# Memory keys and values computed ahead of the first feed-forward, with eleven rooms for the first adaptation pieces and a reordered spatial gate

## The chip, the cores and the metric

The kernel runs on one NeuronCore of a Trainium2 chip. The metric is the device time of one execution in microseconds, and lower is better. Five engines work beside each other, each in the order of its own program, and wait for one another on semaphores: TensorE (PE) multiplies matrices, VectorE (DVE) and ScalarE (ACT) do elementwise work, GpSimd (POOL) prepares and issues the loads of the weights, SyncE (SP) issues the other transfers.

## The reference

The input is x of 512 tokens with 1024 features. Everything is float32.

```
mod = silu(c) @ ada_w + ada_b                    # 1024 -> 6 * 1024: shift, scale and gate, twice
h = rms_norm(x, g) * (1 + sc1) + sh1
p = h @ w_in                                     # inputs and gates of four mixers
merged = sum(gate_i * mixer_i)                   # rwkv7, spatial gating, short convolution, s5
x = x + gt1 * (merged @ w_o)
h = rms_norm(x, g) * (1 + sc2) + sh2
x = x + gt2 * (square(relu(h @ ffn_w1)) @ ffn_w2)     # 1024 -> 4096 -> 1024
x = rms_norm(x, final_g)
for layer in 0, 1:                               # forget attention, then dilated attention with rope
    mn = rmsnorm(mem, norm_mem[layer])           # mem: 256 tokens x 1024, an input
    km, vm = split(mn @ w_mem_kv[layer])         # 4 memory heads of 64, keys and values
    heads = concat(attention of 12 heads over x, attention of 4 heads over km, vm)
    x = x + heads @ w_out[layer]
    x = x + conv_ffn(rmsnorm(x, norm_ffn[layer]))     # 1024 -> 2 * 2816, convolution, 2816 -> 1024
y = rmsnorm(x, norm_final)
```

`mn` depends on the input `mem` and on no `x`.

## The kernel before

Activations lie transposed: features on the 128 partitions, the 512 tokens along the row. A product is made from three matmuls, high half times high half, high times low, and low times high. The weights come as pieces of 128 x 1024 in one stream of 334. A tile is the product of one piece with eight blocks of 128 features: 24 matmuls of 512 columns into one PSUM bank, of which four are in turn. `project(tiles, owner, ...)` issues tiles, and waits for the low half of each piece and for the bank to be read.

The weight stream has four slots. For each piece q, GpSimd waits for the high half, writes its negative to the low slot (L448), issues a load that adds the full weights to it (L451), and then issues the high half of piece q + 2 (L442). That one waits until TensorE has begun piece q - 1. GpSimd does all this in order, so the low half of the next piece is issued behind that wait.

The adaptation weights are 48 pieces of 512 KB, in six groups of eight (`modulate(group, a, b)`, L576 and L578, multiplies and adds pieces on VectorE; `modulation(group)`, L1682, sums over the partitions on TensorE with 8 matmuls of one column). Pieces 0 to 3 are taken by TensorE itself (L1690). Groups 0 and 1 are needed before the first norm, group 2 before the x update, 3 and 4 around it, 5 in the first feed-forward. SyncE loads them in order into rings of rooms: eight rooms for pieces 0 to 15, four later.

In the run-up, VectorE computes the tables of the s5 mixer: `f` as six products of 128 x 1024 (L1009 to L1014), then group 0, the reciprocal, group 1, and the norm (`norm`, L538 and L534). TensorE transposes `f` (L1850) and multiplies it with `c_in` (L1855) before the first `project`. After the first ten tiles (convolution and spatial gate inputs) the spatial gate has a layer norm: sums on TensorE (L1873), a root on ScalarE (L1356), reciprocal and scaling on VectorE (L1103 to L1106), transposes on TensorE (L1879). The short convolution and group 2 stand on VectorE ahead of it, and small s5 tables of up to 512 columns (L1076 to L1092). The s5 scan is fed at L1899 and read at L1912.

Around the first feed-forward: `last_terms(mixer_update)` updates x as the eight w_o tiles end (L1188) with two adaptation multiplies beside each; ScalarE squares (L1266), TensorE sums (L1698), ScalarE takes the root (L1268), VectorE norms.

The memory in each layer: the memory input is loaded, squared and summed beside the last group of the feed-forward before it. Behind the tiles `memq0 memq1 q0 k0 v0` of the attention stand `memk0 memk1 memv0 memv1`, each with 256 columns. VectorE makes their operand in 24 instructions (L836, L483, L484). Values come out transposed, are copied by ScalarE (L1310), turned by TensorE (`turn`, L1711, bank 7) and taken by VectorE (L822). Then `attention(layer)` starts with unit 0, whose scores are the first memory pair (L1782), reduced on VectorE (L890). The attention's 32 units share TensorE with the remaining q, k, v tiles.

## Time and profile before

| | |
|---|---|
| median of 3 runs | 2261.84 us (2259.82 to 2265.03) |
| profiled execution | 2262.56 us, span 2260.7 us |
| mean granted TensorE clock | 0.968 |
| TensorE busy | 2124.0 us (94%) |
| VectorE busy | 1296.8 us (57%) |
| ScalarE busy | 455.7 us (20%) |
| GpSimd busy | 841.6 us (37%) |
| moved by DMA | 389.34 MB, 172 GB/s in the mean |

Busy time says what an engine was occupied with, not that the end depended on it. The chain that ended last, followed back from the end, is 77% TensorE, 14% VectorE and 6% DMA. Durations of matmuls are modelled and overlap: the distance between starts is what one costs. A granted clock of 1.00 is 2.4 GHz, 0.50 is 1.2 GHz.

### The profile page before, as it was taken

Reading aid. Unit: us, or ns where it says so; the run is one execution under the profiler, and the core shown is the slowest. Engines: PE = TensorE matmul, PEld = TensorE weight load, DVE = VectorE, ACT = ScalarE, POOL = GpSimd, SP = SyncE. Lnnn points to the kernel's source line nnn. Section 1 sums busy time; section 2 is a strip of 40 time slices with the busy share of each in tenths; the row PEclk is TensorE's granted clock in tenths of the full one; section 3 lists DMA queues with packets and bytes.
Section 4 is the critical chain, followed back from the end, with each engine's and each line's share of the span. In section 5 each row is a group of like instructions: output and inputs, shape, how many; then the busy total and the mean of one; then the engine's idle time right before and its main releaser. Section 6 shows DMA issues by size and latency. Waiting matters only on the chain.

```text
span 2260.7 us, 27381 instructions
## 1 busy us (share of the span) xinstructions
PE 2124.0 (94%) x10790; PEld 1684.3 (75%) x10790; DVE 1296.8 (57%) x1827; ACT 455.7 (20%) x839; POOL 841.6 (37%) x1009
## 2 busy tenths in 40 slices
PE   6989799998799999998999999999989989999996
PEld 5768587776588888876777888888766768888885
DVE  6775646437653243684444754727746657727374
ACT  2112301220100000313333211202224342202021
POOL 1323233233244444442223444444432224444442
PEclk7999899999799999999999999999999999999998
DMA  8867567579799888875556888988964549889885
GB/s 289 229 139 170 112 142 165 114 168 234 210 241 198 190 193 195 190 170 119 110 103 162 186 192 198 186 197 171 200 135 99 112 90 195 189 196 197 190 187 127
DMA packets 121783, 389.34 MB, mean 172 GB/s; under 512 B 25220, under 2 KB 27396, under 8 KB 121272
## 3 DMA queue, kind: packets, MB, share of 16 engines
q0 software_dynamic: 96624, 346.27, 70.6%
q1 hardware_dynamic: 25032, 41.32, 5.5%
q8 instruction: 86, 1.41, 0.3%
q14 instruction: 41, 0.34, 0.0%
HBM read 383.67 MB, written 3.92 MB: 171 GB/s over the span
## 4 chain that ended last, share of the span: by engine, by line
PE 77%; DVE 14%; DMA 6%; issue 1%; ACT 1%; POOL 0%; SPq 0%; DVEq 0%; ACTq 0%
PE ps L1617 64%; DMA w_lo<-in_w 2%; DMA arena<-in_ada 2%; PE ps L1646 2%; PE ps L1782 2%; PE ps L1811 2%; PE ps L1797 1%; DVE work L690 1%; PE ps L1969 1%; DVE g_lo L484 1%; PE ps L1733 1%; DVE arena L691 1%; DVE arena L578 1%; DMA w_hi<-in_w 1%; DVE small L890 0%
## 5 line engine op out<-in xcount | busy, mean ns | idle before, releaser
L1617 PE MATMUL ps<-h_hi,w_hi 128*128 128x512 f32 x1760 | 711.8, 404 | 27.3 <-DVE h_lo L534 13.1
L1617 PE MATMUL ps<-h_hi,w_lo 128*128 128x512 f32 x1760 | 690.3, 392 | 0.0
L1617 PE MATMUL ps<-h_lo,w_hi 128*128 128x512 f32 x1760 | 690.2, 392 | 0.0
L442 POOL DMA_DIRECT2D w_hi<-in_w x334 | 186.3, 558 | 1218.1 <-PE ps L1617 1082.9
L1617 PEld LDWEIGHTS ps<-h_hi,w_hi 128*128 128x128 f32 x1760 | 333.0, 189 | 125.5 <-issue 29.9
L1617 PEld LDWEIGHTS ps<-h_hi,w_lo 128*128 128x128 f32 x1760 | 332.8, 189 | 71.5
L1617 PEld LDWEIGHTS ps<-h_lo,w_hi 128*128 128x128 f32 x1760 | 333.8, 190 | 65.0 <-issue 2.2
L448 POOL TENSOR_SCALAR w_lo<-w_hi 128x1024 fp32r<-128x1024 f32 (+1 forms) x334 | 355.6, 1065 | 67.1 <-DMA w_hi<-in_w 61.8
L451 POOL DMA_DIRECT2D w_lo<-in_w x334 | 300.9, 901 | 106.0 <-POOL w_lo L448 106.0
L1617 PE MATMUL ps<-g_hi,w_hi 128*128 128x512 f32 (+1 forms) x760 | 297.1, 391 | 10.3 <-DMA w_lo<-in_w 6.3
L1617 PE MATMUL ps<-g_lo,w_hi 128*128 128x512 f32 (+1 forms) x760 | 291.1, 383 | 0.0
L1617 PE MATMUL ps<-g_hi,w_lo 128*128 128x512 f32 (+1 forms) x760 | 291.0, 383 | 0.0
L1617 PEld LDWEIGHTS ps<-g_hi,w_hi 128*128 128x128 f32 x760 | 144.8, 191 | 43.9 <-DMA w_lo<-in_w 9.2
L1617 PEld LDWEIGHTS ps<-g_hi,w_lo 128*128 128x128 f32 x760 | 144.7, 190 | 27.8
L1617 PEld LDWEIGHTS ps<-g_lo,w_hi 128*128 128x128 f32 x760 | 144.9, 191 | 26.6 <-issue 0.5
L1575 ACT ACTIVATE arena<-arena,vec 128x512 f32<-128x512 f32 x88 | 71.8, 816 | 392.1 <-DVE arena L936 388.8
L950 DVE TENSOR_TENSOR x<-ps,x 128x512 f32<-128x512 f32 x48 | 33.2, 692 | 146.0 <-PE ps L1617 135.8
L941 DVE SCALAR_TENSOR_TENSOR arena<-arena,vec 128x511 f32<-128x511 f32 x88 | 114.9, 1305 | 3.3 <-ACT arena L1575 0.3
L936 DVE TENSOR_TENSOR arena<-ps,work 128x512 f32<-128x512 f32 x88 | 60.8, 691 | 90.3 <-PE ps L1617 88.9
L1205 DVE TENSOR_TENSOR arena<-arena 128x512 f32<-128x512 f32 x32 | 54.3, 1696 | 70.6 <-ACT arena L1496 70.6
L1213 DVE SCALAR_TENSOR_TENSOR x<-ps,mod,x 128x512 f32<-128x512 f32 x32 | 24.0, 751 | 101.9 <-PE ps L1617 101.7
L483 DVE CAST g_hi<-arena 128x512 fp32r<-128x512 f32 (+1 forms) x100 | 75.5, 755 | 3.4
(376 smaller groups left out, 2109.3 us busy)
## 6 DMA issues: line engine op xcount, KB each, us to landing
w_hi<-in_w POOLq DMA_DIRECT2D x318, 512.0 KB, 3.9
w_lo<-in_w POOLq DMA_DIRECT2D x318, 512.0 KB, 5.6
arena<-in_ada SPq DMA_DIRECT2D x40, 512.0 KB, 9.4
w_hi<-in_w POOLq DMA_DIRECT2D x16, 384.0 KB, 3.4
w_lo<-in_w POOLq DMA_DIRECT2D x16, 384.0 KB, 5.1
x<-in_ada SPq DMA_DIRECT2D x8, 512.0 KB, 7.9
x<-in_xT SPq DMA_DIRECT2D x1, 2048.0 KB, 9.5
x<-in_xT SPq DMA_DIRECT2D x4, 512.0 KB, 5.3
```

Source lines behind the costliest of these rows:

```text
L442: pool.dma_start(w_hi[:, q % SLOTS, 0:n], A["w"][q][:, 0:n]).then_inc(S(f"high_in{q % SLOTS}"), 16)
L448: pool.tensor_scalar(w_lo[:, q % SLOTS, 0:n], w_hi[:, q % SLOTS, 0:n].bitcast(F32), -1.0, 0.0, ALU.mult, ALU.add).then_inc(S("negated"), 1)
L451: pool.dma_start(w_lo[:, q % SLOTS, 0:n], A["w"][q][:, 0:n], accum_op=ALU.add).then_inc(S(f"low_in{q % SLOTS}"), 16)
L483: do(dve.tensor_copy(hi, src))
L936: do(dve.tensor_tensor(cv_m["z"][:, side, :], tile()[:], rstd, ALU.mult), "conv_scaled")
L941: do(dve.scalar_tensor_tensor(dst[:, 1:], z[:, :T - 1], w(1), dst[:, 1:], ALU.mult, ALU.add))
L1205: do(dve.tensor_tensor(s, r, r, ALU.mult), "relu_used")
L1575: do(act.activation(c[:, j % 2, :], cv_m["z"][:, side, :], ACT.Identity, scale=V("cw2", at), bias=V("cb2", 44 * layer + 22 * side + j0 + j ...
L1617: mm = pe.matmul(bank, w[:, slot, cols], a(k), start=(k == 0 and i == 0), stop=(k == blocks - 1 and i == 2))
L1646: mm = pe.matmul(banks[i], w[:, slots[i], cols], a(k), start=(k == 0 and j == 0), stop=(k == blocks - 1 and j == 2))
L1782: mm = pe.matmul(ps[2 + g][:, 0:width], at_m["q"][half(g), pair, P * qb:P * qb + P], keys, start=True, stop=not fox)
L1811: mm = pe.matmul(ps[6][64 * g:64 * g + 64, P * qb:P * qb + P], values, at_m["pt"][:, u % 2, g, P * b:P * b + P], start=(b == 0), stop=(b = ...
```

## The change

Three things change.

The memory's norm, keys and values of both layers are computed between the x update and the first feed-forward. Eight pieces of `w_mem_kv` move there in the weight stream, and the pieces per layer fall by four. The norm is factored: only the gain is applied to the operand (ScalarE makes the high half, `mem_high`, VectorE the low half, `memory_low`, in `mixer_update`), the root's reciprocal multiplies the keys afterwards (`mem_scaled`, in the first feed-forward group) and the values as they are copied (`mem_row`, its transposed form). Values are computed with the memory as the stationary operand (`memory_values`), so that they come out with tokens on the partitions and are not turned. The memory input is loaded once, behind adaptation pieces 24 to 27.

The first adaptation pieces get eleven rooms; pieces 11 to 15 wait for VectorE to have used the room. The products `f` and the s5 transposes and products move behind the first norm.

The convolution, group 2 of the adaptation and its sum move behind the spatial gate's sums. Group 2's last four pieces are loaded behind the s5 input's transfers.

VectorE, from the s5 tables to the second adaptation group (L10xx are products of 1024 columns, L576 and L578 multiply adaptation pieces, L527 is the norm's reciprocal). Before:

```order
L1012 TENSOR_TENSOR arena<-arena 128x1024
L1013 TENSOR_TENSOR arena<-arena 128x1024
L1014 TENSOR_TENSOR arena<-arena 128x1024
L1033 TENSOR_SCALAR arena<-arena 128x128
L576 TENSOR_SCALAR arena<-arena,small 128x1024
L578 SCALAR_TENSOR_TENSOR arena<-arena,small 128x1024 x3
L580 MEMSET small 128x8
L527 RECIPROCAL work<-work 128x512
L576 TENSOR_SCALAR arena<-arena,small 128x1024
L578 SCALAR_TENSOR_TENSOR arena<-arena,small 128x1024 x7
L580 MEMSET small 128x8
L587 TENSOR_TENSOR mod<-ps,vec 128x16
```

Of the change (L595 and L597 multiply adaptation pieces, L546 is the reciprocal, L557 the norm):

```order
L1007 TENSOR_TENSOR arena<-arena 128x8x4
L595 TENSOR_SCALAR arena<-arena,small 128x1024
L597 SCALAR_TENSOR_TENSOR arena<-arena,small 128x1024 x3
L599 MEMSET small 128x8
L595 TENSOR_SCALAR arena<-arena,small 128x1024
L597 SCALAR_TENSOR_TENSOR arena<-arena,small 128x1024 x7
L599 MEMSET small 128x8
L546 RECIPROCAL work<-work 128x512
L606 TENSOR_TENSOR mod<-ps,vec 128x16
L1032 SCALAR_TENSOR_TENSOR small<-mod,vec 128x8
```

The six products and `c_in`'s sign are gone from this place, and the reciprocal follows the second group.

ScalarE, from the root of the rwkv norm to the first feed-forward tile (L1382 gates, L1266 squares of x, L1268 root, L1274 the norm's high half, L1496 relu). Before:

```order
L1483 ACTIVATE small<-small 128x16
L1382 ACT_TABLE_LOAD
L1382 ACTIVATE arena<-ps 128x512 x4
L1259 ACT_TABLE_LOAD
L1259 ACTIVATE small<-small 128x1
L1266 ACTIVATE work<-x 128x512 x8
L1268 ACTIVATE work<-ps,small 128x512
L1274 ACTIVATE h_hi<-work,mod 128x512 x8
L1496 ACTIVATE arena<-ps 128x512 x25
```

Of the change (L1269 squares of x, L1271 root, L1309 copies keys, L1315 copies values, L1512 the norm's high half, L1524 relu; the 24 activations of the memory norm stand ahead of these rows):

```order
L1262 ACTIVATE small<-small 128x1
L1269 ACTIVATE work<-x 128x512 x8
L1271 ACTIVATE work<-ps,small 128x512
L1309 ACTIVATE arena<-ps 128x256 x2
L1315 ACTIVATE arena<-ps,small 128x256 x2
L1512 ACTIVATE h_hi<-work,mod 128x512 x2
L1309 ACTIVATE arena<-ps 128x256
L1512 ACTIVATE h_hi<-work,mod 128x512 x2
L1309 ACTIVATE arena<-ps 128x256
L1512 ACTIVATE h_hi<-work,mod 128x512 x4
L1315 ACTIVATE arena<-ps,small 128x256 x2
L1524 ACTIVATE arena<-ps 128x512 x32
```

Copies of keys and values now stand between the high halves of the norm.

VectorE, from the memory's last eviction to the first unit of layer 0 (L820 and L822 take turned values, L853 copies keys, L858 to L867 the forget sums, L890 the first score reduction). Before, with the 24 rows of the memory norm ahead of these:

```order
L820 COPY arena<-ps 128x4x128
L853 COPY arena<-ps 128x256
L858 TENSOR_SCALAR work<-work 12x512
L859 TENSOR_TENSOR work<-work 12x512
L860 MEMSET work 12x512
L861 SCALAR_TENSOR_TENSOR work<-work 12x512
L864 CAST work<-work 12x512
L865 TENSOR_TENSOR work<-work 12x512
L866 CAST work<-work 12x512
L867 TENSOR_TENSOR work<-work 12x512
L822 COPY arena<-ps 128x2x128 x2
L890 TENSOR_REDUCE small<-ps 128x2
```

Of the change (L815 the scaled memq0, memq1, q0 and k0, L857 to L866 the forget sums, L832 the scaled v0, L887 the reduction):

```order
L815 SCALAR_TENSOR_TENSOR arena<-ps,work 128x512 x4
L857 TENSOR_SCALAR work<-work 12x512
L858 TENSOR_TENSOR work<-work 12x512
L859 MEMSET work 12x512
L860 SCALAR_TENSOR_TENSOR work<-work 12x512
L863 CAST work<-work 12x512
L864 TENSOR_TENSOR work<-work 12x512
L865 CAST work<-work 12x512
L866 TENSOR_TENSOR work<-work 12x512
L832 TENSOR_TENSOR arena<-ps,work 128x512
L887 TENSOR_REDUCE small<-ps 128x2
L893 RECIPROCAL small<-small 128x2
```

Nothing of the memory is left between the scaled tiles and the first reduction.

```diff
-ADA_PE, ADA_FIRST = 4, 8
+ADA_PE, ADA_FIRST = 4, 11
...
             for q in range(16):
-                if ADA_FIRST <= q < ADA_FIRST + ADA_PE:
-                    sp.wait_ge(S("ada_taken"), q - ADA_FIRST + 1)
-                elif q >= ADA_FIRST + ADA_PE:
-                    sp.wait_ge(S("ada_used"), q - ADA_FIRST - ADA_PE + 1)
-                sp.dma_start(first_slots[q % ADA_FIRST], A["ada"][q]).then_inc(S(ada_landed(q)[0]), 16)
+                if q >= ADA_FIRST:
+                    sp.wait_ge(S("ada_used"), q - ADA_FIRST + (3 if q == 15 else 1))
+                sp.dma_start(first_slots[first_room(q)], A["ada"][q]).then_inc(S(ada_landed(q)[0]), 16)
...
+            for q in range(16 + ADA, 24):
+                ada_piece(q, ada_second["ada"])
...
             def memory_root():
+
                 need("rms_ready")
                 do(dve.reciprocal(mem_rstd, mem_rstd))
+                for i in range(2):
+                    do(dve.tensor_tensor(mem_m["diag"], mem_rstd[:, P * i:P * i + P], K("ident"), ALU.mult))
+                    do(dve.tensor_reduce(mem_row[:, i:i + 1], mem_m["diag"], AX.X, ALU.add), "mem_row")
+
+            def memory_low(i):
+
+                layer, k = i // KT, i % KT
+                need("mem_high")
+                do(dve.scalar_tensor_tensor(mn(g_lo, layer, k), mem_in[:, k, :], V("g_mem2", 8 * layer + k), mn(g_hi, layer, k).bitcast(F32),
+                                            ALU.mult, ALU.subtract), "mem_ready")
...
-                value_scaled("v0")
-                for i in range(NMP):
-                    do(dve.tensor_copy(km[:, i, :], tile()[:, 0:MT]), "dve_freed")
-                    if i == 0:
-                        value_taken("v0")
                 if layer == 0:
                     need("forget_log")
                     do(dve.tensor_scalar(f(0), f(0), 0.0, None, ALU.min))
@@ -865,9 +864,7 @@
                     do(dve.tensor_tensor(f(3), f(4), f(0), ALU.subtract))
                     do(dve.tensor_copy(part(1), f(3)))
                     do(dve.tensor_tensor(part(2), f(3), f(1), ALU.subtract), "forget_parts")
-                skip(2)
-                for i in range(NMP):
-                    value_taken(f"memv{i}")
+                value_scaled("v0")
 
...
-            do(dve.tensor_scalar(c_in[:, 1], c_in[:, 1], -1.0, None, ALU.mult), "s5_f")
             n.next("square", KT)
             n.next("square_used", KT)
             modulate(0, ADA_PE, 8)
+            modulate(1, 0, 8)
             norm_start()
-            modulate(1, 0, 8)
             modulation(0, 2)
             gain1 = small[:, 2, :]
             do(dve.scalar_tensor_tensor(gain1, mod[:, 8:16], 1.0, V("g_mix", 0, 8), ALU.add, ALU.mult))
             norm(lambda k: gain1[:, k:k + 1], lambda k: mod[:, k:k + 1])
...
 
             skip(4)
-            modulation(2)
             need("sg_sums")
             d = m["z"][:, 2:4, :]
             do(dve.tensor_scalar(m["mu"], PA[:], 1.0 / DM, None, ALU.mult))
             for k in range(2):
                 do(dve.tensor_tensor(d[:, k, :], d[:, k, :], m["mu"], ALU.subtract))
                 do(dve.tensor_tensor(m["sq"][:, k, :], d[:, k, :], d[:, k, :], ALU.mult), "sg_square")
...
+            convolved(1)
             shifted(1)
             for k in range(2):
                 need("sg_mixed")
...
 
             count = [0]
 
@@ -1161,6 +1155,9 @@
             do(dve.tensor_tensor(w[:, 1, :], w[:, 1, :], w[:, 3, :], ALU.add), "s5_states")
             for i in range(3, 7):
                 shifted(i)
+                if i < 6:
+                    modulate(2, 2 * (i - 2), 2 * (i - 2) + 2)
+            do(dve.tensor_tensor(mod[:, 16:24], tile()[:, 0:8], V("ada_b", 16, 8), ALU.add), "dve_freed")
...
             def mixer_update(k):
                 do(dve.scalar_tensor_tensor(x[:, k, :], tile()[:], mod[:, 16 + k:17 + k], x[:, k, :], ALU.mult, ALU.add), "x_done")
+                for i in range(3 * k, min(3 * k + 3, 2 * KT)):
+                    memory_low(i)
+                if k == 2:
+                    memory_root()
...
-                    if last:
-                        add_square(j, mem_sq, mem_total)
+                    if first and j < 2 * NMP:
+                        keys = mem_keys[j // NMP][:, j % NMP, :]
+                        dve.wait_ge(S("mem_copied"), 2 * N_KV)
+                        do(dve.tensor_tensor(keys, keys, mem_rstd, ALU.mult), "mem_scaled")
                 if first:
                     modulation(5)
                 update = lambda k: do(dve.scalar_tensor_tensor(x[:, k, :], tile()[:], mod[:, 40 + k:41 + k], x[:, k, :],
...
+            for k in range(KT):
+                if k >= MEM_SQ:
+                    act.wait_ge(S("mem_square_used"), k - MEM_SQ + 1)
+                do(act.activation(mem_sq(k), mem_in[:, k, :], ACT.Square), "mem_square")
+            act.wait_ge(S("tile"), n.value["tile"])
+            for layer in range(2):
+                for k in range(KT):
+                    do(act.activation(mn(g_hi, layer, k), mem_in[:, k, :], ACT.Identity, scale=V("g_mem2", 8 * layer + k)), "mem_high")
+            act.wait_ge(S("mem_square_used"), KT)
+            do(act.activation(mem_rstd, PB[:, 0:MT], ACT.Sqrt, bias=small[:, 38, 0:1], scale=1.0 / D), "rms_ready")
             skip(8)
             rms_x(0)
-            high_shifted(lambda k: mod[:, 24 + k:25 + k])
+            for i in range(NMP):
+                keys_copy(0, i)
+            values_copy(0)
+
+            def high2(k):
+                need("norm_scaled")
+                do(act.activation(h_hi[:, k, :], work[:, 4 + k % 2, :], ACT.Identity, bias=mod[:, 24 + k:25 + k]), "h_high")
+
+            for k in range(KT):
+                high2(k)
+                if k in (1, 3):
+                    keys_copy(1, k // 2)
+            values_copy(1)
             for g in range(FF_GROUPS):
...
+            def memory_values(layer):
+
+                at = [bank_of(t[0] + i) for i in range(2)]
+                for b in at:
+                    pe.wait_ge(S(freed[b][0]), freed[b][1])
+                for k in range(KT):
+                    if k % 4 == 0:
+                        slot = open_piece()
+                    hi, lo = mn(g_hi, layer, k), mn(g_lo, layer, k)
+                    cols = slice(MT * (k % 4), MT * (k % 4) + MT)
+                    for i in range(2):
+                        tokens = slice(P * i, P * i + P)
+                        for j, (a, w) in enumerate(((hi, w_hi), (hi, w_lo), (lo, w_hi))):
+                            mm = pe.matmul(ps[at[i]][:, 0:NMP * P], a[:, tokens], w[:, slot, cols], start=(k == 0 and j == 0),
+                                           stop=(k == KT - 1 and j == 2))
+                            if k % 4 == 0 and i == 0 and j == 0:
+                                mm.then_inc(S("w_used"), 1)
+                        if k == KT - 1:
...
-                    mm = pe.transpose(ps[i][:, P * s:P * s + P], m["f"][:, i // 2, 4 * (i % 2) + s, :], K("ident"))
+                    mm = pe.transpose(ps[4 + i][:, P * s:P * s + P], m["f"][:, i // 2, 4 * (i % 2) + s, :], K("ident"))
                 mm.then_inc(S("s5_turned"), 1)
+            project(1, "dve_freed")
+            pe.wait_ge(S("s5_e"), 4)
             for s in range(S5T):
                 for part in range(2):
                     for g in range(2):
                         mm = pe.matmul(ps[6 + g][:, 16 * s:16 * s + 16], m["f"][halves[g], part, s, :], m["c_in"][halves[g], part, s, :],
                                        start=(part == 0), stop=(part == 1))
             mm.then_inc(S("s5_products"), 2)
-            modulation(0)
-            modulation(1)
-            pe.wait_ge(S("s5_e"), 4)
-            project(10, ["dve_freed"] * 6 + ["act_freed"] * 4, ready=h_tile)
-            modulation(2)
+            project(6, ["dve_freed"] * 2 + ["act_freed"] * 4)
 
...
             branch_out(3, 8)
+            for k in range(KT):
+                pe.wait_ge(S("mem_square"), k + 1)
+                pe.matmul(PB[:, 0:MT], K("ones"), mem_sq(k), start=(k == 0), stop=(k == KT - 1)).then_inc(S("mem_square_used"), 1)
             project(7, "x_done", ready=lambda k: need("merged"))
             modulation(3)
             project(1, "x_done")
+            memory = [(lambda k: mn(g_hi, 0, k), lambda k: mn(g_lo, 0, k)), (lambda k: mn(g_hi, 1, k), lambda k: mn(g_lo, 1, k))]
+            pe.wait_ge(S("mem_ready"), 2 * KT)
+            project(1, "mem_copied", operand=memory[0], width=MT)
             modulation(4)
+            total_squares(work[:, 2, :])
+            project(NMP - 1, "mem_copied", operand=memory[0], width=MT)
+            memory_values(0)
+            project(NMP, "mem_copied", operand=memory[1], width=MT)
+            memory_values(1)
             g = (of(g_hi), of(g_lo))
             hidden = lambda k: need("hidden")
-            total_squares(work[:, 2, :])
             for group in range(FF_GROUPS):
                 project(8, "hidden_relu", ready=h_tile if group == 0 else None)
                 project(2, "x_done", operand=g, ready=hidden)
                 if group == 0:
...
                 project(1, "v_scaled")
                 if layer:
                     turn("k0", layer)
-                project(1, "dve_freed", operand=mem, width=MT, ready=lambda k: need("mem_ready"))
-                turn("v0", layer)
-                project(NMP - 1, "dve_freed", operand=mem, width=MT)
-                for i in range(NMP):
-                    project(1, "v_copied", operand=mem, width=MT)
-                    if i:
-                        turn(f"memv{i - 1}", layer)
-                turn(f"memv{NMP - 1}", layer)
-                attention(layer)
+                attention(layer, ready)
...
```

## Rows read from the trace of the kernel before

**Rows 1.** The chain that ended last, in order of time (start us, us, what)

```profile
168.35 2.08 PE ps L1899 x64
...
185.05 3.72 PE ps L1912 x64
...
490.72 8.18 DMA w_lo<-in_w
...
666.11 261.30 PE ps L1617 x1152
...
1005.84 4.67 PE ps L1617 x24
```

**Rows 2.** Timeline of DVE, 20 to 50 us (start, us, instruction, idle before)

```profile
20.30 1.23 DVE L1009 TENSOR_TENSOR arena<-arena 128x1024 f32<-128x1024 f32 x1
...
48.80 1.63 DVE L578 SCALAR_TENSOR_TENSOR arena<-arena,small 128x1024 f32<-128x1024 f32 x1 [1.42 <-DMA arena<-in_ada]
```

**Rows 3.** DMA rate, 0 to 60 us in 40 slices

```profile
GB/s 0 204 377 327 328 360 385 396 415 415 418 426 404 366 76 14 22 284 169 224 235 249 336 265 317 371 394 360 276 259 391 356 237 266 374 258 206 186 182 193
```

**Rows 4.** PE: its waits in total (us, times, longest), and timeline, 30 to 146 us

```profile
PE ps L1617 <- DMA w_lo<-in_w: 12.0, 10, 2.0
...
32.27 3.66 PE L1850 MATMUL ps<-con,arena 128*128 128x128 f32 x16
35.85 7.01 PE L1855 MATMUL ps<-arena 64*128 64x16 f32 x64
...
119.89 1.84 PE L1682 MATMUL ps<-con,work 128*128 128x1 f32 x16
...
141.82 3.78 PE L1873 MATMUL ps<-arena,con 128*128 128x512 f32 x4 [7.28 <-DVE arena L1101]
```

**Rows 5.** Timeline of DVE, 103 to 184 us

```profile
103.02 0.49 DVE L1062 TENSOR_SCALAR arena<-arena,vec 128x512 f32<-128x512 f32 x1
...
112.71 0.69 DVE L484 TENSOR_TENSOR g_lo<-arena,g_hi 128x512 fp32r<-128x512 f32 x1
...
139.33 0.07 DVE L1092 MEMSET arena<- 128x8 f32 x1
...
183.01 0.69 DVE L1161 TENSOR_TENSOR arena<-arena 128x512 f32<-128x512 f32 x1
```

**Rows 6.** Busy time by stretch (us; PE, PEld, DVE, ACT, POOL; PEclk, DMA, GB/s)

```profile
587.00:615.30 28.30, 16.60 (x42) 10.15 (x43) 21.65 (x26) 7.09 (x10) 2.50 (x3) 0.58 0.48 136
545.00:587.00 42.00, 40.03 (x181) 32.29 (x179) 28.68 (x29) 4.44 (x7) 16.93 (x20) 0.99 1.02 309
```

**Rows 7.** Timeline of ACT, 596 to 616 us

```profile
596.49 0.69 ACT L1268 ACTIVATE work<-ps,small 128x512 f32<-128x512 f32 x1 [8.06 <-PE ps L1698]
...
615.56 0.60 ACT L1496 ACTIVATE arena<-ps 128x512 f32<-128x512 f32 x1 [1.97 <-PE ps L1617]
```

**Rows 8.** Timelines of POOL and PE, 1643 to 1654 us

```profile
1643.39 0.56 POOL L442 DMA_DIRECT2D w_hi<-in_w  x1 [4.97 <-PE ps L1617]
...
1651.09 0.39 PE L1617 MATMUL ps<-g_hi,w_hi 128*128 128x256 f32 x1 [1.64 <-DMA w_lo<-in_w]
...
1653.94 0.28 PE L1617 MATMUL ps<-g_hi,w_lo 128*128 128x256 f32 x1
```

**Rows 9.** Timelines of PE and DVE, 997 to 1022 us

```profile
997.78 0.28 PE L1617 MATMUL ps<-g_hi,w_hi 128*128 128x256 f32 x1
...
1011.06 1.77 DVE L858 TENSOR_SCALAR work<-work 12x512 f32<-12x512 f32 x1
...
1018.02 0.68 DVE L867 TENSOR_TENSOR work<-work 12x512 fp32r<-12x512 f32 x1
...
1021.73 0.69 DVE L890 TENSOR_REDUCE small<-ps 128x2 f32<-128x512 f32 x1 [1.48 <-PE ps L1782]
```

**Rows 10.** Timelines of PE and DVE, 1634 to 1658 us

```profile
1634.13 1.02 PE L1708 MATMUL ps<-arena,con 128*128 128x512 f32 x2
...
1657.16 0.69 DVE L890 TENSOR_REDUCE small<-ps 128x2 f32<-128x512 f32 x1 [1.09 <-PE ps L1782]
```

199 lines of the change are left out of this document (97 added, 102 removed).

## The prediction

> **What bounds the kernel now.** I read the chain of waits in order of time first. Long stretches of it are nothing but TensorE: 1152 matmuls of 512 columns in 261.3 us, so 0.227 us each and 5.44 us for a tile of 24 [rows 1]. There the time is fixed, and only pieces taken out of the program could shorten it. The change takes none out of these stretches; it moves work between the places where TensorE waits. So the sum is made from the waits, place by place, with the timelines of the engines beside each other. Four places matter: the run-up to the first norm, the gap before the first feed-forward, and the starts of the two attentions.
>
> **A. First norm.** VectorE computes six products of 1024 columns from 20.30 to 27.9 us before it touches the first adaptation piece; the last multiply starts at 48.80 and waited for its DMA [rows 2]. In the data rates of the first 60 us the DMA falls idle once (76, 14, 22 GB/s at slices 15 to 17 of 1.5 us), and runs at 240 to 430 else [rows 3]: with eight rooms pieces 8 to 11 wait for TensorE to have taken pieces 0 to 3. With eleven rooms nothing waits there, and since the products move behind the norm, rooms 4 to 7 come free from about 22 us. Bytes that must have moved by the last piece: 8.4 MB of pieces, 2.1 of x, 1.4 of constants, and 1.6 of weights that come between; 13.5 MB at some 390 GB/s from 3 us on end near 38 us, and with the multiply the sum stands at 39.5 instead of 50.4: 11 us earlier. Bounds: VectorE alone (12 multiplies of 1.3 from 20.3) would give 36, so 14 us; the old ring's pace gives 45, so 5.
>
> What TensorE did while it waited now stands between tiles: 16 transposes (3.66) and 64 small products (7.01) [rows 4], both at the half clock level in that row's stretch; warm I take half, 5.4 us. TensorE's waits for low halves are ten in the whole program, 12.0 us, the longest 2.0 [rows 4]; two of them lay here, 1.9 us, and can go, since only four of the eight next adaptation pieces still compete. The tenth tile ended at 119.9, where the adaptation sum starts [rows 4]: 119.9 - 11 + 5.4 - 1.9 = 112.4.
>
> **Spatial gate.** TensorE waited 7.28 us at 141.82 for VectorE, and ran the sums in 3.78, the half level [rows 4]. VectorE was late because two convolutions (103.0 to 113.4, 5.2 each) and eight adaptation multiplies stood ahead of its 26 us of small tables, which ended at 139.3 [rows 5]. Without them it ends near 117. So TensorE goes 112.4, tile, 1.9 us of sums, tile, 1.9 us of sums: 127.1 where it was 145.6, 18.5 ahead. The root, reciprocal and transposes follow as before; the second convolution (5.2) now stands ahead of the mixing, and I find VectorE done with it at 150.0 where TensorE's scan inputs started at 168.35 [rows 1], 18.2 ahead. Given back: two multiplies (2.4) go ahead of the scan, of which 1.3 is covered (VectorE's last step ended at 183.7, TensorE used it at 185.05 [rows 1, 5]), and the adaptation sum, 1.84 [rows 4], moves behind. **A = -15.3 us**, between -9 and -19.
>
> **B. Memory input.** 1 MB more is queued near 487 us, where the load of a low half takes 8.18 us on the chain [rows 1]: +1. Eight squares are summed on TensorE. Two sums of 512 columns took 3.78 at the half level [rows 4], so eight of 256 warm take 3.8 us. They run while the first w_o tile waits for its merged parts, and cost nothing; without that cover, +3.8. ScalarE and VectorE work of this norm (24 activations, 16 subtractions) lies beside the update of x, where VectorE is busy 28.7 of 42 us and the DMA share is 1.02 [rows 6]; 10 us more just fits. If it doesn't, up to 3 us, kept in the range.
>
> **C. The memory pieces before the feed-forward.** TensorE is busy 16.6 of the 28.3 us from 587.0 to 615.3, at a granted clock of 0.58 [rows 6]. The adaptation sums and the squares are done when ScalarE takes the root at 596.49, and the first feed-forward tile is read at 615.56 [rows 7]. Eight short pieces now go in. One takes 2.9 us warm (1651.09 to 1653.94 and its own 0.28) [rows 8]. TensorE's need is thus 23 us, and would nearly fit. But the weights do not come so fast: GpSimd asks for a high half at 1643.39 when a piece begins, only then issues the next low half, and TensorE waits until 1651.09 for it [rows 8]. With 0.5 us from the piece's start to the issue, a piece starts no sooner than 8.2 us after the piece two before it. Piece 0 starts at 587.0, piece 1 behind the adaptation sum and the squares at 596.4, then 599.3, 604.6, 607.5, 612.8, 615.7, 621.0, and the first feed-forward tile at 623.9. ScalarE copies the results out in between and its last normed part is ready near 623, so that tile runs at full pace and ends at 629.3. **C = +14 us.** Bounds: 0, if the feed keeps up and fully hides; +22, if cold (below).
>
> **D. Attention, layer 0.** TensorE had the last value tile at 997.78; the first score reduction on VectorE was at 1021.73 [rows 9]. In between lay four memory pieces, 24 norm steps and two transposed copies. What is late next: VectorE's forget sums, 1011.06 to 1018.70, 7.6 us [rows 9], now directly behind the fourth scaled tile. That tile ends near 992.4, so 993.3 + 7.6 + 0.7 for the value tile = 1001.8: 19.9 earlier. The value's four transposes (0.9, a quarter of the 16 in 3.66 [rows 4]) move into the attention, where TensorE is the bound. **D = -19.0.** If the value tile's eviction made the attention's tiles wait, -16.
>
> **E. Attention, layer 1.** The second rotation ran on TensorE at 1634.13; the first reduction was at 1657.16 [rows 10]. Now rotation (2.2) and value scaling (0.7) follow it, and the reduction comes at 1637.6: 19.5 earlier, less 0.9. **E = -18.6**, at least -15.
>
> **F.** Two sums of squares of 256 columns go, 0.5 us each by the same row: **-1**. Masks and rope tables keep their places in the DMA queue.
>
> **Sum.** -15.3 + 1 + 14 - 19.0 - 18.6 - 1 = -38.9. The profiled execution took 2262.56, 1.9 more than its span; 2262.56 - 38.9 = **2224**. The median of the three runs is 2261.84, 0.7 less; I leave it at that.
>
> **Rivals.** *Cold feed.* The short pieces run at the half level: 24 of them took 4.67 us with part at half level [rows 1], 5.1 if all. Then seven pieces from 596.4 end at 632.1, and the next tile at 638: C = 22.5, time 2232. For it: a granted clock of 0.58 in that stretch. Against: after a wait of 1.64 us the piece at 1651.09 ran at full level [rows 8]. The Trainium skill, "TensorE: Matmul & The Clock Gate", section "HAM oscillation — how this bites in real kernels", says that bursts shorter than the weight waits between them start cold every time. By that rule C is this rival's; by the row it is mine. The row at 1651.09 speaks against the rule so far, and its stretch had fewer waits than this one will.
>
> *The front gives little.* The last adaptation piece lands at 45 and VectorE remains last at the scan: A = -5, time 2234. For it: the weights' first loads compete at 40 us. Against: the idle slices.
>
> *Memory fully hidden.* The feed keeps TensorE's pace, C = 0: 2210. Against: the 1.64 us that a short piece waited for its low half [rows 8].
>
> *Slower.* In C nothing overlaps: each of six pieces from 599.3 on pays the 8.2 of the feed, its own 2.9, and 0.5 more, since with adaptation pieces on the DMA a low half alone can take 8.18 us [rows 1]. At 11.6 a piece the first feed-forward tile starts at 668.9 and ends at 674.3: C = +59, time 2269. It decides from 10.6 us a piece, where C eats the other 52.9. For it: the last adaptation pieces load just then, 4 MB. Against: the low half asked for after 1643.39 was there at 1651.09 though the one before it had been on its way [rows 8], so two overlap.
>
> **Chances.** Forecast 0.55 (alone 2216 to 2231), cold feed 0.15, weak front 0.12, hidden 0.12, slower 0.04; 0.02 that it all comes to nothing. The range takes the hidden case's edge and both middle rivals: 2208 to 2242. Less than 0.2% (4.5 us) cannot be told from no change. Faster 0.94, same 0.02, slower 0.04.
>
> **What would show it.** The last adaptation multiply ends near 39.5; the wait of 7.28 for VectorE is gone; the scan inputs start near 150. Between the last update of x and the first feed-forward tile TensorE runs eight short pieces with waits for low halves of 2 to 3 us before every second one, and the second feed-forward tile starts 14 us later in relation to the x updates. The first score reduction follows the last value tile's end by some 4 us in both layers. It is wrong if the stretches between (feed-forward, down products, recurrence) change their lengths, or if the attentions take longer than 1.1 us more each.

## The result and the profile after

| | before | after |
|---|---|---|
| first comparison, medians | 2260.83 us (4 runs) | 2243.31 us (2242.19 to 2249.14, 4 runs) |
| ratio | | 0.9928, interval 0.9902 to 0.9953 |
| second comparison | 2265.17 us (9 runs) | 2241.46 us (2240.33 to 2244.40, 4 runs) |
| ratio | | 0.9896, interval 0.9882 to 0.9910 |
| profiled executions | 2262.56 us | 2249.14 and 2240.72 us |

The change is faster by 17 to 24 us. The forecast was 38 us, and its range ended at 2242, below the first median and above the second. The sign was right; the size forecast was 1.6 to 2.2 times the measured one.

The page of the changed kernel, its first profiled execution:

```profile
span 2247.3 us, 27332 instructions
PE 2122.3 (94%) x10794; PEld 1686.9 (75%) x10794; DVE 1273.4 (57%) x1778; ACT 462.0 (21%) x850; POOL 844.9 (38%) x1009
DMA packets 121639, 388.29 MB, mean 173 GB/s; under 512 B 25204, under 2 KB 27380, under 8 KB 121256
```

Bytes and shares are nearly those of before (1.05 MB less, since the memory input is loaded once), so they do not tell where the time went; the chain of waits does. The chain of after, in order of time (start us, us, what), to be read against [rows 1]:

```profile
155.44 2.08 PE ps L1949 x64
172.17 3.72 PE ps L1962 x64
482.59 11.10 DMA w_lo<-in_w
493.73 7.32 PE ps L1633 x24
604.14 8.22 DMA w_lo<-in_w
615.03 7.65 DMA w_lo<-in_w
625.72 7.22 DMA w_lo<-in_w
691.00 293.94 PE ps L1633 x1296
```

The reader is to see two things. The scan inputs (168.35 before) start 12.9 us earlier, and the long run of the feed-forward (666.11 before) starts 24.9 us later. Between them stand four loads of low halves. The 1296 matmuls of that long run take 293.94 us, 0.227 each as before.

By stretches, each measured between the same two events of TensorE in both traces (us; the last column is the change once more):

| stretch | before | after | difference | forecast | again |
|---|---|---|---|---|---|
| start to the solve's first product behind its DMA (A) | 377.56 | 368.16 | -9.4 | -15.3 | -14.1 |
| to the recurrence's last product | 108.80 | 110.07 | +1.3 | 0 | +0.2 |
| to the output's transposes, past the low half near 490 (B) | 18.25 | 22.76 | +4.5 | +1 | +5.7 |
| to the adaptation's last sum (C) | 86.29 | 91.41 | +5.1 | 0 | +4.9 |
| to the adaptation sum in the feed-forward (C) | 73.37 | 96.76 | +23.4 | +14 | +21.5 |
| to the sum of squares ahead of layer 0's feed-forward (D) | 581.44 | 557.39 | -24.1 | -19.5 | -24.2 |
| to that of layer 1 (E) | 640.43 | 624.39 | -16.0 | -19.1 | -16.5 |
| to the end | 374.56 | 376.36 | +1.8 | 0 | +0.6 |

The forecast's F is split over D and E. The stretches of the two layers gave together what was forecast: -40.1 against -38.6. The start gave 3.5 us less in the mean of its two executions (the thirteen profiled kernels with this start stand between -7.1 and -14.1 at this event, -10.3 in the mean). The stretch around the memory pieces cost 28.5 and 26.4 us where 14 stood, and B 3.5 and 4.7 more than forecast. That is nearly all of the miss.

The memory pieces on TensorE, their first matmuls, and the first feed-forward tile (start us, us, instruction, idle before):

```profile
592.40 3.58 PE L1701 MATMUL ps<-con,arena 128*128 128x1 f32 x16 [7.68 <-DVE small L599]
596.90 1.20 PE L1633 MATMUL ps<-g_hi,w_hi 128*128 128x256 f32 x1
601.54 0.28 PE L1737 MATMUL ps<-w_hi,g_hi 128*128 128x256 f32 x1
612.40 0.39 PE L1633 MATMUL ps<-g_hi,w_hi 128*128 128x256 f32 x1 [3.32 <-DMA w_lo<-in_w]
622.82 0.36 PE L1737 MATMUL ps<-w_hi,g_hi 128*128 128x256 f32 x1 [2.65 <-DMA w_lo<-in_w]
632.99 0.50 PE L1633 MATMUL ps<-h_hi,w_hi 128*128 128x512 f32 x1 [2.70 <-DMA w_lo<-in_w]
```

The second piece starts at 596.90, the first feed-forward tile at 632.99: 36.1 us for seven pieces (35.8 in the other execution), 10.2 to 10.9 for two. Before, that tile began at 603 and its result was read at 615.56 [rows 7]; now ScalarE reads it 24.9 us later:

```profile
640.46 0.60 ACT L1524 ACTIVATE arena<-ps 128x512 f32<-128x512 f32 x1 [9.43 <-PE ps L1633]
```

GpSimd in that stretch: the high half that waits for the piece at 601.54, the negation of the next piece, and the issue of its low half, which lands at 612.36. Below it is the busy time from 612 to 623 and in the whole row of pieces (us; PE, PEld, DVE, ACT, POOL; PEclk, DMA share, GB/s):

```profile
602.13 0.55 POOL L450 DMA_DIRECT2D w_hi<-in_w  x1 [0.88 <-PE ps L1737]
602.70 1.14 POOL L456 TENSOR_SCALAR w_lo<-w_hi 128x1024 fp32r<-128x1024 f32 x1
604.14 0.89 POOL L459 DMA_DIRECT2D w_lo<-in_w  x1 [0.30 <-POOL w_lo L456]
...
612.00:623.00 11.00, 7.88 (x49) 7.41 (x50) 6.28 (x8) 3.37 (x6) 5.02 (x6) 0.84 1.00 206
601.50:633.00 31.50, 21.40 (x147) 20.32 (x145) 15.38 (x18) 8.82 (x15) 15.11 (x18) 0.89 0.95 204
```

The order of the steps is the forecast's. The landing is not: 8.22, 7.65 and 7.22 us where [rows 8] showed 5.7. The DMA engines are busy nearly all the time (share 0.95, and 1.00 from 612 to 623) at only 204 to 206 GB/s.

VectorE in the attentions' heads, the first score reduction in layer 0 and in layer 1, answering [rows 9] and [rows 10]:

```profile
1025.28 0.69 DVE L887 TENSOR_REDUCE small<-ps 128x2 f32<-128x512 f32 x1
...
1639.32 0.69 DVE L887 TENSOR_REDUCE small<-ps 128x2 f32<-128x512 f32 x1
```

### The profile page after: what moved, and what is told of

Same layout as the page of the kernel before. It is cut to its first block, busy times and chain, and to the rows that moved or that the text cites. A ratio compares the mean times of both kernels' runs of the same rounds, so it can differ in the third digit from the quotient of the medians.

```text
span 2247.3 us, 27332 instructions
## 1 busy us (share of the span) xinstructions
PE 2122.3 (94%) x10794; PEld 1686.9 (75%) x10794; DVE 1273.4 (57%) x1778; ACT 462.0 (21%) x850; POOL 844.9 (38%) x1009
## 3 DMA queue, kind: packets, MB, share of 16 engines
q0 software_dynamic: 96624, 346.27, 72.4%
## 4 chain that ended last, share of the span: by engine, by line
PE 79%; DVE 10%; DMA 7%; issue 1%; ACT 1%; POOL 1%; SPq 0%; DVEq 0%; ACTq 0%
PE ps L1633 65%; DMA w_lo<-in_w 4%; PE ps L1662 2%; PE ps L1830 2%; PE ps L1859 2%; PE ps L1845 1%; DMA w_hi<-in_w 1%; DMA arena<-in_ada 1%; PE ps L2020 1%; DVE work L709 1%; PE ps L1778 1%; POOL w_lo L456 1%; DVE arena L710 1%; DMA x<-in_xT 1%; PE ps L1701 1%
## 5 line engine op out<-in xcount | busy, mean ns | idle before, releaser
L1633 PE MATMUL ps<-g_hi,w_hi 128*128 128x512 f32 (+1 forms) x728 | 287.2, 395 | 8.7 <-DMA w_lo<-in_w 7.8
L1633 PE MATMUL ps<-g_lo,w_hi 128*128 128x512 f32 (+1 forms) x728 | 282.2, 388 | 0.0
L1633 PE MATMUL ps<-g_hi,w_lo 128*128 128x512 f32 (+1 forms) x728 | 282.1, 387 | 0.0
L1633 PEld LDWEIGHTS ps<-g_hi,w_hi 128*128 128x128 f32 x728 | 138.3, 190 | 42.5 <-DMA w_lo<-in_w 11.9
L1633 PEld LDWEIGHTS ps<-g_hi,w_lo 128*128 128x128 f32 x728 | 138.5, 190 | 27.9
L1633 PEld LDWEIGHTS ps<-g_lo,w_hi 128*128 128x128 f32 x728 | 138.6, 190 | 27.0 <-issue 0.8
L1524 ACT ACTIVATE arena<-ps 128x512 f32<-128x512 f32 x32 | 19.1, 597 | 292.0 <-PE ps L1633 292.0
```

The costliest lines, as they stand in the source:

```text
L1633: mm = pe.matmul(bank, w[:, slot, cols], a(k), start=(k == 0 and i == 0), stop=(k == blocks - 1 and i == 2))
```

## The experiments

Theories. **Loads**: from the second memory piece to the first feed-forward tile the DMA engines' time per piece sets the pace. **TensorE**: its short pieces at the half clock level do (the cold feed of the prediction). **Chain**: fixed delays of GpSimd's order (issue, negation, issue, landing) do. A chain in which the landing itself grows with the load on the DMA engines is no rival of the first theory but its other side, and no run here parts the two. Beside them stand smaller questions on the start, on B, and on the adaptation's late sum. All comparisons are ratios to the kernel before on the same chip; four kernels at a time shared one. Where positions inside a kernel are compared, each comes from one profiled execution. Medians separate few of these kernels: of the ten variants of the change below, only the interval of the one named `both_stag` and that of the last one lie apart from the change's (0.9882 to 0.9910).

### The change again, and the start alone

> The changed kernel once more, for a second profile and a second comparison. Its first profiled execution was 2249.14 us, 5.8 above the median of 2243.31, so some places in it were late by chance. Expected: median near 2243, with the memory stretch (the second memory piece to the first feed-forward tile) again near 36.1 us, and the last tiles of layer 1, which stood 4.4 us later against the attention's start than before, without that loss.

Measured: 0.9896 (0.9882 to 0.9910), 2241.46 us. The memory stretch 35.8 us. The loss behind the second attention's start was there again: 3.5 us from there to the end, where 4.4 were lost in the first trace, so most of it was no chance. The expectation was wrong in this. Most of it lies in layer 1's attention; the part on D and E below has the numbers.

The start alone; group 2's sum now takes a tile of its own, so the tiles behind it count one more:

```
# before.py with the change's hunks for the start only, and
-    first_beside = n_block1 + small_extra + 1 + len(HEAD_PIECES)
+    first_beside = n_block1 + small_extra + 2 + len(HEAD_PIECES)
```

> The kernel before with the start alone changed: eleven rooms, the products behind the norm, the spatial gate's sums ahead of the convolution, group 2 late. The memory is computed where it was. Theory: the gain of the start stays to the end as the trace of the changed kernel has it behind the solve (369.05 against 378.45), so -8 to -9.5 us in the median. Rival: the gain is given back at waits for weights and adaptation pieces around 490 to 590, which do not come earlier, and -3 or less is left. The memory's part is what remains of -17.5 after this: about -8.5 by the theory, -15 by the rival.

Measured: 0.9948 (0.9934 to 0.9961), 2254.45 us beside 2265.17, 10.7 less. The start's gain stays: -8.6 at the solve, -7.9 at the adaptation sum in the feed-forward, -6.8 at the end of the span. The rival falls. What the memory's move brings is the rest: 2254.45 - 2241.46 = 13 us, where the prediction had 23.6.

### What sets the pace of the memory pieces

Each part of a piece's cost was taken away by itself. The three kernels of this section leave out part of the memory's work, so their keys and values are not the right ones; they only price it. First TensorE's work:

```
-            project(NMP, "mem_copied", operand=memory[1], width=MT)
+            project(NMP, "mem_copied", operand=memory[1], width=MT, blocks=1)
# the same for layer 0; in memory_values: for k in (0, 4)
```

> The changed kernel, where TensorE does 3 of the 24 products of each memory piece for the keys and 6 of 24 for the values (the loads and waits stay; keys and values lack the rest). Theory (the loads set the pace): two pieces still take about 10 us, and what is gained is what TensorE does in the last two of them, 2 to 5 us. Rival (TensorE at the half clock level is the bound): 15 us or more.

Measured: 0.9889 (0.9853 to 0.9925). The pieces and the first feed-forward tile on TensorE, and the busy time of the stretch:

```profile
594.57 0.41 PE L1737 MATMUL ps<-w_hi,g_hi 128*128 128x256 f32 x1
602.14 0.58 PE L1737 MATMUL ps<-w_hi,g_hi 128*128 128x256 f32 x1 [6.09 <-DMA w_lo<-in_w]
607.78 0.58 PE L1633 MATMUL ps<-g_hi,w_hi 128*128 128x256 f32 x1 [3.99 <-DMA w_lo<-in_w]
618.23 0.55 PE L1737 MATMUL ps<-w_hi,g_hi 128*128 128x256 f32 x1 [5.70 <-DMA w_lo<-in_w]
628.87 0.79 PE L1633 MATMUL ps<-h_hi,w_hi 128*128 128x512 f32 x1 [4.81 <-DMA w_lo<-in_w]
...
597.00:630.00 33.00, 8.06 (x27) 6.43 (x28) 14.44 (x18) 8.43 (x14) 15.94 (x20) 0.50 0.96 211
```

TensorE works 8.06 of 33 us, and two pieces still take 10.4 to 10.6 (607.78, 618.23, 628.87). From the second piece, at 593.14, to the feed-forward tile it is 35.7 us, as with the change. Nothing that can be measured was gained, less than either theory asked. TensorE and its clock are not the bound. Half of the bytes:

```
-                n = piece_cols.get(q, D)
+                n = 512 if n_mixer + 8 <= q < n_mixer + 16 else piece_cols.get(q, D)   # both loads
```

> The changed kernel, where the two loads of each of the eight memory pieces bring 512 of the 1024 columns (the products read what lies in the rest; GpSimd's negation and every wait stay). Theory (the DMA engines are full in this stretch, about 4.9 us of them for the 1 MB of a piece): two short pieces take some 7 us in place of 10.4, and the first feed-forward tile comes 9 to 11 us earlier. Rival (a chain of fixed delays: issue, negation, issue, landing): two pieces still take 9.5 or more, and at most 3 us are gained.

Measured: 0.9866 (0.9819 to 0.9913). The second piece and the feed-forward tile, and the median landings of the two sizes from 595 to 635 us (those of 512 KB belong to the feed-forward):

```profile
590.62 1.20 PE L1634 MATMUL ps<-g_hi,w_hi 128*128 128x256 f32 x1
618.73 0.50 PE L1634 MATMUL ps<-h_hi,w_hi 128*128 128x512 f32 x1 [1.88 <-DMA w_lo<-in_w]
...
w_lo<-in_w POOLq DMA_DIRECT2D x5, 512.0 KB, 7.5
w_lo<-in_w POOLq DMA_DIRECT2D x4, 256.0 KB, 4.5
```

28.1 us for seven pieces: 8.0 less. Counted from the output's transposes the tile comes 10.6 to 11.1 us earlier, within the 9 to 11 expected, as the adaptation's last sum comes 2.7 earlier too. Delays that don't depend on the bytes can't be the bound, so the chain theory falls as it was put. The engines are no longer full here: their share is 0.84 from 595 to 618 us, and TensorE is busy 18.6 of these 23. Is it the adding?

```
-                pool.dma_start(w_lo..., accum_op=ALU.add)
+                pool.dma_start(w_lo..., **accumulate)        # no accum_op for the eight pieces
```

> The changed kernel, where the low half of the eight memory pieces is loaded without adding (the low half then holds the full weights). Theory A (it is the adding that is dear; the high half lands in 5.6 us and the low half in 7.2): the low half lands in some 5.5, two pieces take 8.5, and 5 to 7 us are gained. Theory B (the bytes alone count): no difference, within 1.5 us.

Measured: 0.9863 (0.9828 to 0.9898). From 587.01 to 618.79, 31.8 us: 4.3 less than with the adding. From the output's transposes to the adaptation sum in the feed-forward it is 181.1 us, 5 to 7 less, as expected. The seven low halves issued from 586 to 620 us land in 5.0 in the median, where it was 7.2. The DMA view of these 34 us, and a window of it:

```profile
q0 software_dynamic: 1928, 7.00, 74.8%
...
596.00:617.00 21.00, 15.96 (x115) 15.18 (x114) 12.50 (x15) 8.45 (x14) 11.80 (x15) 0.92 0.80 222
```

74.8% of 34 us for 7.00 MB is 3.6 us a MB, where the change's trace has 4.6 (below). Theory A holds: of the same bytes, those that are added take more of the DMA engines. At a share of 0.80 the engines are not full in this kernel, so its gain is not the whole price of the adding. The intervals of these three kernels' ratios overlap with one another and with the change's, so it is their traces that show the differences, not the medians.

### The low half without its load

```
+                if first_short <= q < first_short + 8:
+                    pool.tensor_tensor(w_lo[...], w_hi[...].bitcast(F32), w_lo[...].bitcast(F32), ALU.add)
+                    return                     # in place of the load that adds
```

> The changed kernel, where the low half of the eight memory pieces is not loaded: GpSimd adds the high half's tile, which holds the full weights, to the negated one (a second operation of 128 x 1024 behind the negation, which takes 1.06 us). The results are the same; 4 MB of 8 are no longer moved. Theory (DMA engine time per byte sets the pace): the memory stretch falls from 36 to 25 to 28 us as with half the bytes, and 8 to 10 us are gained. Rival (GpSimd's own work and its order set the pace, or the addition slows VectorE): two pieces still take 9 us or more, and at most 4 us are gained.

Measured: 0.9890 (0.9870 to 0.9909), 2240.94 us: nothing gained. GpSimd's two operations for one piece, the first feed-forward tile, and the busy time of the stretch:

```profile
608.06 1.06 POOL L456 TENSOR_SCALAR w_lo<-w_hi 128x1024 fp32r<-128x1024 f32 x1
609.20 2.72 POOL L461 TENSOR_TENSOR w_lo<-w_hi,w_lo 128x1024 fp32r<-128x1024 f32 x1
...
632.55 0.58 PE L1642 MATMUL ps<-h_hi,w_hi 128*128 128x512 f32 x1 [4.52 <-DMA w_lo<-in_w]
...
597.00:630.00 33.00, 27.69 (x186) 25.87 (x186) 23.34 (x18) 7.52 (x13) 24.94 (x20) 0.87 0.47 131
```

The DMA share falls to 0.47, so the loads are off the path, and GpSimd takes their place: with the issue 4.1 to 4.4 us a piece, without a pause from 603.3 to 626.5. From the second piece at 601.66 to the tile it is 30.9 us, 5 less than with the change, though this includes a wait of 4.52 for the tile's own low half, which could only be issued behind the additions. The rival is right in its mechanism. Ahead of these pieces 2.8 us were lost: the adaptation's last sum came at 597.15, 94.1 us behind the output's transposes instead of 91.3. What is left, 2.0 to 2.5 us at the tile, does not show in the median.

### The early piece and the late subtractions

```
-            project(1, "mem_copied", ...); modulation(4); total_squares(...); project(NMP - 1, "mem_copied", ...)
+            project(NMP, "mem_copied", ...); modulation(4); total_squares(...)
```

> The changed kernel with the second memory piece ahead of the adaptation's last sum, and nothing else changed. Theory (the loads' pace counts from the first piece): one piece's load time, 4 to 5 us, is gained. Rival (the pace is set by something behind the root, the norm or the copies): nothing.

Measured: 0.9872 (0.9835 to 0.9908). The piece ran at 586.54, the feed-forward tile at 623.32; from the output's transposes to the adaptation sum in the feed-forward it is 183.5 us, 186.1 to 188.2 with the change. 2.6 to 4.7 us less, about what the loads' pace gives for one piece; the comparison of medians alone does not show it. From the second piece to the tile it is 36.8 us, though the adaptation's sum and the squares now stand in between: the row of loads keeps its length.

```
-                for i in range(3 * k, min(3 * k + 3, 2 * KT)):       # 16 subtractions beside updates 0 to 5
+                for i in ((0, 1), (2, 3), (4, 5), (6, 7), (12,), (13,), (), ())[k]:   # six behind the last multiply;
+                                                    # the waits for mem_high and mem_ready follow this order
```

> The changed kernel with six of layer 1's subtractions behind VectorE's last adaptation multiply, TensorE's order as it was. Theory (VectorE's 16 subtractions made the last adaptation multiply late: 5 us from the output sums on, against 0.4 with the start changed alone): the adaptation's last sum comes 3 to 4 us earlier, and as much is gained. Rival (the adaptation pieces' loads are what is late, the DMA share there is 1.03): under 1.5 us earlier.

Measured: 0.9886 (0.9866 to 0.9906). The last sum on TensorE:

```profile
586.60 3.33 PE L1705 MATMUL ps<-con,arena 128*128 128x1 f32 x16 [3.31 <-DVE small L599]
```

It is 88.7 us behind the output's transposes, where it was 91.4 and 91.2 with the change and 86.3 before. So the subtractions' place is worth 2.6 of the 5 us, a little under the 3 to 4 expected, and the median shows no gain (0.9886 beside the change's 0.9896). The subtractions are not the only cause: with lighter memory loads and the subtractions where they were, the sum came at 88.6 (half of the bytes) and 88.1 (no adding). The memory's weights beside the adaptation pieces delay it as well. Both orders together:

> The changed kernel with two orders altered around the first feed-forward. The second memory piece goes ahead of the adaptation's last sum, into 7.7 us in which TensorE waited. Six of layer 1's subtractions move behind VectorE's last adaptation multiply. Theory (the loads of the short pieces set the pace from the first to the last of them, 10.2 to 10.9 us for two): a piece that starts 12 us earlier starts the loads behind it earlier, and the second feed-forward tile, at 640.5 now, comes 9 to 12 us earlier. Rival (the norm's end at 628.1 sets the first feed-forward tile as soon as the loads don't): 4 to 5 us earlier, no more.

Measured: 0.9883 (0.9866 to 0.9900), 2238.43 us beside 2241.46, which the intervals do not part. From the output's transposes to the sum in the feed-forward 180.2 us, 6 to 8 less than the change, and under the 9 to 12 expected. VectorE's last multiply no longer sets the sum: the early piece does, whose low half is there at 586.50 and which runs 4.5 us.

### B: 2.5 MB ahead of a low half

```
-            for q in range(24, 24 + ADA): ada_piece(q, ...)
-            sp.dma_start(mem_in, A["memT"])
+            sp.dma_start(mem_in, A["memT"]); sp.wait_ge(S("mem_in"), 16)
+            for q in range(24, 24 + ADA): ada_piece(q, ...); sp.wait_ge(landed(q))
```

> As the one with both orders altered, and near 480 us the memory input is loaded ahead of the first four adaptation pieces of group 3, and each of these is issued when the one before it has landed. Theory (2.5 MB issued at once in front of a low half made TensorE wait until 493.7, with a landing of 11.1 us): the low half there lands in 7 us or less, and 3 to 4 us are gained on top. Rival: these adaptation pieces now land late for VectorE at the x update, or the low half takes as long since the bytes are the same; no gain, up to 2 us lost.

Measured: 0.9861 (0.9848 to 0.9875), 2233.47 us, 5 below the kernel with both orders, whose interval overlaps. B's stretch is 17.8 us where the change has 22.8 and 23.9 and before 18.25: the wait and the half-level tile are gone. Not all of the 5 us are B's. The kernel with both orders had 20.6 there, so 2.8 were won; the stretch from the transposes to the feed-forward's sum took 1.7 back (181.9 for 180.2), and 2.5 were won at the solve already, where the edit has not acted yet.

> The changed kernel with the stagger near 480 us alone. Theory: the wait for the low half there (2.5 to 3.0 us) and the tile at half clock level behind it (1.6 to 2.8) go, 3 to 5 us. Rival: the adaptation pieces come later to VectorE at the update of x, and take back 2 us or more of it.

Measured: 0.9901 (0.9878 to 0.9925), 2243.78 us: no gain in the median. B fell to 19.5, and the rival took its share: the adaptation's last sum came 93.4 us behind the transposes, 2.1 later than with the change. Over all profiled kernels, B is 20.6 to 23.9 us in the nine that have the change's loads there, and 17.8 to 19.5 in the three with the stagger.

### All together

> The addition in place of the low half's load, with the second piece early, six subtractions late and the adaptation pieces staggered. Theory (each takes away another part: 5 us per piece that starts early, 3 to 5 us near 480, 8 us of load time): 8 to 12 us below the one with both orders and the stagger (2233.5), near 2223. Rival (with the loads gone the norm's end sets the first feed-forward tile, so the early piece brings nothing more): as the addition alone with the stagger's 4 us, near 2229.

Measured: 0.9849 (0.9827 to 0.9871), 2232.28 us beside 2267.14. Its median is the lowest, 35 us below the kernel before, but it is not 8 to 12 below the one without the addition: its interval and that one's (0.9848 to 0.9875) overlap. The first feed-forward tile waits 4.63 us for its load, as with the addition alone. The addition brings nothing that can be measured; what is gained over the change is there without it.

## Why the prediction was wrong

**What failed is one term, C, and in it one step**: "With 0.5 us from the piece's start to the issue, a piece starts no sooner than 8.2 us after the piece two before it." The form was right: piece by piece, every second one waits for its low half. The 8.2 was not: it rests on a landing of 5.7 us, read in a stretch in which one short piece waited once [rows 8]. In a row of short pieces the loads meet one another, and the landing is 7.2 to 8.2. From the piece at 601.54 it is 0.6 us to the high half's issue, 2.0 to the low half's and 8.2 to its landing, 10.9 in place of 8.2; from one waiting piece to the next it is 10.2 to 10.9. The row that should have priced it is that of the load's own cost in DMA time, not its latency: in the DMA view of 595 to 635 us, the queue of the weights has

```profile
q0 software_dynamic: 1989, 7.28, 84.4%
```

84.4% of 40 us for 7.28 MB is 4.6 us a MB, 4.9 for a piece of 1.05 MB. Seven such pieces are 34 us; 36.1 were measured. The trace of before had the same price in its queue (4.20 MB in 47% of the same 40 us, 4.5 us a MB, and 346.27 MB in 70.6% of the whole span, 4.6), and a full tile of 5.44 hides it with half a microsecond to spare. (The Trainium skill, "DMA: Bandwidth & Descriptors", section "Specifications", gives some 358 GB/s as the limit between the HBM and one core. By that, as an estimate, a piece would be 2.9 us, as short as its products, and the feed would keep up; the trace stays far below the limit, with 206 GB/s at a share of 1.00.)

**C, the rest.** Of the 14.5 us that are missing, 8.6 are this pace (36.1 against 27.5), 5.1 the adaptation's last sum, and 1.8 the first feed-forward tile, which took 7.2 for 5.44 behind its wait; the squares stood 1.0 closer than forecast. For the last sum the prediction said "10 us more just fits" for VectorE, kept 3 us in the range and none in the value. The row gave 28.7 of 42 us busy and a DMA share of 1.02 [rows 6], but over half of VectorE's 13.3 us of idle time there was waits for adaptation pieces (7.6 us in the trace of before), and those pieces are loaded into rooms that VectorE frees. Work put into such idle time can delay the next load.

**The cold-feed rival** came near the size for a wrong reason: it had 22.5, and the stretch behind the last sum cost 23.4 and 21.5. That is luck. The granted clock was 0.84 from 612 to 623, and behind a wait of 3.3 us the matmuls of the piece at 612.40 took 0.41 us in place of 0.28 from the tenth on; yet with TensorE almost idle, at 0.50, the pace was the same. (The Trainium skill, "TensorE: Matmul & The Clock Gate", section "HAM oscillation — how this bites in real kernels", has bursts that are shorter than the waits for their data start cold each time. With TensorE's work taken away, three or six matmuls between waits of 2.6 to 6.1 us, the trace agrees: each took 0.41 or more. The change's own pieces are no such case, since two of them lie between the waits: in the first execution they went on at 0.28 to 0.39 for nine matmuls behind the wait of 3.3 us, in the second they were at 0.41 and more for 14 behind a wait of 2.3.)

**The slower rival** priced a piece at 11.6 us with nothing overlapping; 5.2 was measured, and two loads do overlap. Its remark that 4 MB of adaptation pieces load just then is wrong: the DMA view of 595 to 635 shows 0.52 MB beside the weights.

**A.** The first norm did what was forecast: the first normed tile started 11.05 us earlier (57.28, 46.23), with the added transposes and products at 5.65 for 5.4. "Two of them lay here, 1.9 us, and can go" failed in this execution: the low half asked for at 87.40 landed at 98.14, and

```profile
98.18 0.80 PE L1633 MATMUL ps<-h_hi,w_hi 128*128 128x512 f32 x1 [2.37 <-DMA w_lo<-in_w]
```

the tiles behind it started at the half level (four in 23.63 us, 21.8 at full). These 2.4 and 1.8, and about 1 for another tile that began at the half level at 140, are the 5.3 us by which the scan was late (-12.9 for -18.2). In the second execution the wait was absent and the scan came 16.0 us earlier. The wait of 7.28 for VectorE went as forecast.

**B.** The forecast of +1 looked at the bytes alone; 4.5 and 5.7 were measured. The low half took 11.10 us, and the tile behind it 7.32 for 5.74.

**D and E** were right at the heads. The reduction came 20.9 us earlier within its layer (19.9 forecast) and 18.6 (19.5). Behind them one of the prediction's own signs of being wrong showed, that an attention takes over 1.1 us more. From the first reduction to the sum of squares ahead of the feed-forward, layer 1 took 231.6 and 231.9 us where it was 229.0 before. Layer 0 took 221.3 and 221.2 where it was 224.0, so the two nearly cancel. With the start changed alone layer 1 stood at 230.5. No run looked for the cause; it stays open.

**The range.** It allowed +22 for C and -9 for A. Both together, with B at 4.5, give 2262.56 - 9 + 4.5 + 22 - 38.6 = 2241.5, its very edge. The weak start, the dear pieces and B were treated as alternatives; in the first execution they came together. In the second the start was near its forecast, and the time, 2240.72, was inside the range.

## What to carry to other kernels

In this kernel, and likely in others with such a stream: before short products are moved into idle time of TensorE, price them by the DMA engines' time for their weights (share of the queue times the stretch, over its MB), not by TensorE's time and not by the latency of one load. A weight stream whose full tiles hide 4.9 us in 5.44 has no room for short ones anywhere but where TensorE waits for something else, and there the early start of the first counts, as each piece starts the load behind it. An engine that is idle because it waits for loads into rooms that it must free itself is not free: with six of 16 subtractions taken out of such time on VectorE, the sum behind them came 2.6 us earlier.

## What the hardware showed

- Loads that add cost more DMA time than plain ones of the same size: the queue took 3.6 us a MB with plain low halves and 4.6 with adding ones, and seven pieces 31.8 and 36 us; a low half landed in 5.0 against 7.2 us in the median.
- With all DMA engines busy (share 1.00) such a stream moved 206 GB/s, while [rows 3] has up to 426 in the run-up.
- GpSimd's addition of two 128 x 1024 tiles took 2.4 to 3.3 us, its negation of one 1.06 in the median. (The Trainium skill, "GPSIMD Engine Reference", section "4.1 Engine selection", has operations with two inputs about twice as slow as on VectorE; VectorE's product of two such tiles took 1.23 [rows 2], and the trace agrees.)
- Single waits for weights come and go with the same code: thirteen profiled executions with one start differ by 7.0 us at the solve, and nine with the same loads near 490 us by 3.3 us in that stretch.
